# Seven block products for eight in a feed-forward projection: 8 of 22 tile pairs of the gate and up projections in Strassen's form

## The chip, the cores and the metric
The kernel runs on one core of one Trainium2 chip. The metric is the device time in microseconds of one execution. TensorE (PE) multiplies, with its weight loads shown as PEld; VectorE is DVE, ScalarE is ACT, GpSimd is POOL, and SyncE (SP) issues most of the DMA transfers.

## The reference
A token mixer block and a second block follow each other on 512 tokens of width 1024. The second block holds the two feed-forward layers that the change touches. For each:

```python
def swiglu(h, w_gu, w_down):
    gu = h @ w_gu                      # 1024 -> 2 x 2816
    g, u = jnp.split(gu, 2, axis=-1)
    return (jax.nn.silu(g) * u) @ w_down

f = swiglu(rmsnorm(h, ffn1_pre_g[l]), ffn1_w_gu[l], ffn1_w_down[l])
h = h + 0.5 * rmsnorm(f, ffn1_post_g[l])
```

Everything is float32. `rmsnorm(x, g)` multiplies x by the reciprocal root of its mean square plus 1e-6 and by the gain g.

## The kernel before
**Layout.** Features lie on the 128 partitions, the 512 tokens in the free dimension. A weight is cut into blocks of 128 by 128. All weights stream through *slots* of 8 blocks (`w_raw`, a ring of 6): a slot holds the blocks of one output tile of 128 features. SP loads slot c once slot c-6 has been used on PE (`s_used`).

**Three terms.** Each float32 product is made as three reduced ones: ACT copies a slot to its high part (`split_hi`, `w_hi`, a ring of 4, so it waits for the use of slot c-4), DVE subtracts for the low part, in place of the raw slot (`split_lo`, `w_lo`), and PE adds high by high, high by low and low by high (`gemm`). The tokens have such parts too (`act_hi`, `act_lo`: `HH`, `HL`). The rstd of a row is not in them: it is multiplied in when a tile leaves PSUM (`RP`, `pre_rstd`).

**The feed-forward layer.** `ffn1_up` has 44 slots: gate tile t is slot 2t, up tile t slot 2t+1, for t from 0 to 21. Slots 0 to 2 and half of 3 are multiplied while the boundary before still makes the tokens (`after_boundary`); from slot 4 on PE goes through the slots one by one, with four banks in turn (`ACC[0]`, `ACC[1]`, then `PS[0]`, `PS[1]`). After each tile DVE multiplies by the rstd (L1558), ACT applies silu to the gate tile (L911), DVE multiplies gate by up (L1564) into a ring of two, ACT makes the high part (L633) and DVE the low part (L1185) of the hidden tile. `ffn1_down`, 24 slots, reads them. The second layer (`ffn2`) is the same code.

**Order.** Each engine has its own queue, written out in program order, with semaphores between. DVE and ACT split each slot three slots ahead of PE (`AHEAD = HI_RING - 1`), in `stage`:

```python
for s in range(COUNT[name]):
    if s >= split and base + s + AHEAD < N_SLOTS:
        split_lo(base + s + AHEAD)
    m = tile_ended(name, s)
    if tile is not None and m is not None and (per is None or s % per == per - 1):
        if arrived is not None:
            dve.wait_ge(arrived, at + m + 1)
        tile(m if per is None else s // per)
```

`Chain.link` makes DVE wait until the instruction just issued has ended.

Of the kernel before, what the change touches and what calls it, by code (L numbers as in the profile page):

```python
# [8 lines left out]
F32 = mybir.dt.float32  # L9
F32R = mybir.dt.float32r  # L10
ACT = mybir.ActivationFunctionType
ALU = mybir.AluOpType
# [128 lines left out]
START = [(0, (0, 1, 2)), (1, (0, 1, 2)), (0, (3, 4)), (1, (3, 4)), (2, (0, 1, 2, 3, 4))]  # L141
START += [(s, (k,)) for k in range(5, DK) for s in range(TOGETHER)]


# [58 lines left out]
def block_program(nc, xT, mem_t, w_all, params, consts, rope, decay, w_gate, w_dt, w1k, w1v, w2k, w2v, out_t):  # L203
    ctx = ExitStack()
    with ctx:
# [104 lines left out]
        AH = place("ffn_hi", [P, FK, S], 32, F32R)  # L310
        AL = place("ffn_lo", [P, FK, S], 76, F32R)

        QKV = place("sb_qkv", [P, SB_RING * 3, S], 32)
# [285 lines left out]
        def _(act):  # L599
# [88 lines left out]

            def mixer_root(name, at):

                act.wait_ge(s_rsum, ROWS[name] + 1)
                for c in range(at.start, at.stop):
                    ins = A(RQ[:, c:c + 1], PS[5][:, c:c + 1], ACT.Sqrt, scale=1.0 / D, bias=EPA[:, c:c + 1])
                ins.then_inc(s_rroot, 1)

            def boundary(b, name, gain, next_gain, following):

                slots = tail_slots(name)
                post_root = mixer_root if name == "out2" else row_root
                post_root(f"post{b}", at=chunks(0))  # L700
# [50 lines left out]
            act.wait_ge(s_in, 48)  # L751
            A(WGH[:], WGR[:], ACT.Copy).then_inc(sem("gate_w_hi"), 1)
            row_root("pre")
# [150 lines left out]
            def ffn(n):  # L904
                up = f"ffn{n}_up"

                def tile(t):
                    if t % 2:
                        product_hi(PROD0[f"ffn{n}"] + t // 2, AH[:, t // 2, :])
                    else:  # L910
                        A(ev(up, t), ev(up, t), ACT.Silu).then_inc(sem("gate_made"), 1)  # L911
                stage(up, tile, 2, s_acc)
                branch(f"ffn{n}_down", f"g_ffn{n}_post")
# [3 lines left out]
            for s in range(COUNT["sb_qkv"]):  # L917
                if s >= 2:
                    split_hi(base + s + AHEAD)
                if s == 3:  # L920
                    act.wait_ge(s_late["dt_w"], 16)
                    A(WDH[:], WDR[:], ACT.Copy).then_inc(sem("dt_w_hi"), 1)
# [216 lines left out]
            ffn(2)  # L1139
            row_root("post4", at=chunks(0))  # L1140
            late_squares("ffn2_down")
            late_gains("ffn2_down", "g_ffn2_post")
            row_root("post4_late", at=chunks(1))


        @block.vector
        def _(dve):
# [187 lines left out]
            split_lo(3)  # L1335
            dve.wait_ge(sem("gate_w_hi"), 1)
            TT(WGL[:], WGR[:], WGH[:].bitcast(F32), ALU.subtract).then_inc(sem("gate_w_lo"), 1)
            row_rstd("pre")
# [72 lines left out]
            def first_maxima():  # L1411
# [13 lines left out]
                chain.link(V.memset(PTC[:], 0.0))  # L1425
                dve.wait_ge(sem("gate_rows"), 1)
                TT(NROWS[0:24, :], PS[5][0:24, :], RP[0:24, :], ALU.mult).then_inc(sem("gate_rows_copied"), 1)
                dve.wait_ge(sem("cmp_done"), 1)
# [125 lines left out]
            def ffn(n):  # L1554
                up = f"ffn{n}_up"

                def tile(t):
                    TT(ev(up, t), acc_bank(up, t)[:], RP[:], ALU.mult).then_inc(s_acc, 1)  # L1558
                    if t % 2:
                        j = PROD0[f"ffn{n}"] + t // 2  # L1560
                        free_product(j)
                        dve.wait_ge(sem("gate_made"), 2 * DK + (n - 1) * FK + t // 2 + 1)
                        dve.wait_ge(s_acc, TILE0[up] + t + 1)
                        TT(PR[:, j % 2, :], ev(up, t - 1), ev(up, t), ALU.mult).then_inc(s_pr, 1)  # L1564
                        low(j, AH[:, t // 2, :], AL[:, t // 2, :])
                stage(up, tile, split=2, arrived=s_used)
                branch(f"ffn{n}_down")
# [11 lines left out]
            for s in range(COUNT["sb_qkv"]):  # L1579
# [4 lines left out]
                if s == 4:  # L1584
                    V.memset(ACR[:].bitcast(F32), 0.0)
                    V.memset(SEL[:].bitcast(F32), 0.0)
                    dve.wait_ge(sem("dt_w_hi"), 1)
                    TT(WDL[:], WDR[:], WDH[:].bitcast(F32), ALU.subtract).then_inc(sem("dt_w_lo"), 1)
                if s == 6:
                    dve.wait_ge(sem("dt_rows"), 1)  # L1590
                    TT(NROWS[0:SSD_HEADS, :], PS[2][0:SSD_HEADS, :], RP[0:SSD_HEADS, :], ALU.mult).then_inc(
                        sem("dt_rows_copied"), 1)
                if s == 8:
# [259 lines left out]
        def _(pe):  # L1853
# [74 lines left out]

            def after_boundary(b, branch, name, between=None):

# [17 lines left out]
                row_spread(f"pre{b}", PS[3])  # L1948
                gemm(name, TOGETHER, HH, HL, half=1, h=1)
                for s in range(TOGETHER + 1, COUNT[name]):  # L1950
# [111 lines left out]
            def first_scores():  # L2062

                pe.wait_ge(sem("gate_w_lo"), 1)
                narrow_rows(5, WGH, WGL, 24, range(0, 2))
# [13 lines left out]
                ins.then_inc(sem("cmp_hidden"), 1)  # L2079
                narrow_rows(5, WGH, WGL, 24, range(7, DK)).then_inc(sem("gate_rows"), 1)  # L2080
                pe.wait_ge(sem("cmp_gelu"), 2)
# [8 lines left out]
                ins.then_inc(sem("cmp_done"), 1)  # L2090
                pe.wait_ge(sem("gate_rows_copied"), 1)
                token_major(5, 24).then_inc(sem("gate_psum"), 1)
# [92 lines left out]
            def ffn(n, entered, left, branch):  # L2185
                after_boundary(entered, branch, f"ffn{n}_up")
                down = f"ffn{n}_down"

# [6 lines left out]
            def dt_steps(s):  # L2195
                if s == 6:
                    pe.wait_ge(sem("dt_w_lo"), 1)
                    narrow_rows(2, WDH, WDL, SSD_HEADS).then_inc(sem("dt_rows"), 1)
                if s == 7:
                    pe.wait_ge(sem("dt_rows_copied"), 1)  # L2200
                    token_major(4, SSD_HEADS).then_inc(sem("dt_psum"), 1)
# [406 lines left out]
```

## Time and profile before

| what | value |
|---|---|
| median of 3 runs | 1956.94 us (1956.7 to 1958.17) |
| profiled execution, its own time | 1958.82 us |
| its span, first to last instruction | 1957.1 us |
| mean granted clock of TensorE | 0.997 |
| PE busy | 1916.5 us, 98% |
| DVE busy | 1110.1 us, 57% |
| ACT busy | 859.0 us, 44% |
| first feed-forward, up projection from slot 4 | starts at 589.69 us |

The span and the busy times are of one profiled execution. Matmuls are pipelined: their recorded durations overlap, so what one costs is read from the distance of the starts. The granted clock is a share of full speed.

### The profile page before, as it was taken

To read this page: it belongs to the slowest core of one execution; us is meant where nothing else is said; L and a number is where in the kernel's file an instruction comes from. 1 tells how busy PE (TensorE), PEld (TensorE's weight loads), DVE (VectorE), ACT (ScalarE), POOL (GpSimd) and SP (SyncE) were. 2 spreads that over 40 slices of the span, in tenths; PEclk is the share of its full clock that TensorE was granted. 3 is DMA by queue.
4 is the path that set the end of the run, shared out by engine and by line. 5 is a ranking of instruction groups with operands and counts; after the bars stand their busy time and mean duration, and the time that the engine had idled before them with its cause. 6 is when DMAs were issued, how large, how long until landed. Compare 5 with 4: busy or idle time off the path is not lost.

```text
span 1957.1 us, 25607 instructions
## 1 busy us (share of the span) xinstructions
PE 1916.5 (98%) x10256; PEld 1568.7 (80%) x10256; DVE 1110.1 (57%) x1825; ACT 859.0 (44%) x1532; POOL 91.1 (5%) x109
## 2 busy tenths in 40 slices
PE   8999999999999999999999999999999999999997
PEld 6688877888888888888878887878898888888886
DVE  5678845644465444422738989884745475444323
ACT  4355632533343222322527777974535453222321
POOL 0100000000020000000200000111200020000000
PEclk9999999999999999999999999999999999999999
DMA  7211122333323333333222221122252223333331
GB/s 277 67 55 45 54 70 61 88 99 89 101 63 111 96 97 94 91 90 91 89 80 71 65 66 54 55 87 87 56 157 89 78 86 97 97 91 90 92 96 62
DMA packets 49431, 170.53 MB, mean 87 GB/s; under 512 B 5520, under 2 KB 8080, under 8 KB 48928
## 3 DMA queue, kind: packets, MB, share of 16 engines
q1 hardware_dynamic: 48816, 166.73, 28.4%
q0 software_dynamic: 496, 2.16, 0.3%
q8 instruction: 81, 1.33, 0.3%
q14 instruction: 38, 0.31, 0.1%
HBM read 166.77 MB, written 2.10 MB: 86 GB/s over the span
## 4 chain that ended last, share of the span: by engine, by line
PE 87%; DVE 9%; ACT 2%; issue 1%; DMA 0%; SPq 0%; DVEq 0%
PE acc L1887 54%; PE bank L1887 19%; PE acc L2040 2%; PE bank L1976 2%; DVE w_lo L1160 1%; PE acc L2411 1%; PE bank L2253 1%; PE bank L2160 1%; PE bank L2224 1%; DVE bank L1240 1%; PE bank L2398 1%; PE bank L2432 1%; PE bank L2013 1%; DVE residual L1246 1%; PE bank L1901 1%
## 5 line engine op out<-in xcount | busy, mean ns | idle before, releaser
L1160 DVE TENSOR_TENSOR w_lo<-w_raw,w_hi 128x1024 fp32r<-128x1024 f32 (+2 forms) x306 | 366.5, 1199 | 327.9 <-ACT w_hi L609 327.4
L1887 PE MATMUL acc<-act_hi,w_hi 128*128 128x512 f32 (+1 forms) x1096 | 430.2, 393 | 17.4 <-DVE w_lo L1160 9.5
L1887 PE MATMUL acc<-act_lo,w_hi 128*128 128x512 f32 (+1 forms) x1096 | 419.4, 383 | 0.0
L1887 PE MATMUL acc<-act_hi,w_lo 128*128 128x512 f32 (+1 forms) x1096 | 416.5, 383 | 0.0
L609 ACT ACTIVATE w_hi<-w_raw 128x1024 fp32r<-128x1024 f32 (+2 forms) x306 | 314.5, 1029 | 192.7 <-PE acc L1887 162.7
L1887 PEld LDWEIGHTS acc<-act_hi,w_hi 128*128 128x128 f32 x1096 | 206.4, 188 | 64.5 <-issue 13.2
L1887 PEld LDWEIGHTS acc<-act_hi,w_lo 128*128 128x128 f32 x1096 | 205.9, 188 | 44.5 <-issue 1.2
L1887 PEld LDWEIGHTS acc<-act_lo,w_hi 128*128 128x128 f32 x1096 | 206.6, 189 | 43.1 <-issue 2.2
L1887 PE MATMUL bank<-act_hi,w_hi 128*128 128x512 f32 (+1 forms) x520 | 192.6, 370 | 1.2 <-DVE w_lo L1160 1.2
L1887 PE MATMUL bank<-act_hi,w_lo 128*128 128x512 f32 (+1 forms) x520 | 191.0, 367 | 0.0
L1887 PE MATMUL bank<-act_lo,w_hi 128*128 128x512 f32 (+1 forms) x520 | 190.9, 367 | 0.0
L1887 PE MATMUL acc<-ffn_hi,w_lo 128*128 128x512 f32 (+1 forms) x352 | 134.2, 381 | 0.0
L1887 PE MATMUL acc<-ffn_lo,w_hi 128*128 128x512 f32 (+1 forms) x352 | 134.2, 381 | 0.0
L1887 PE MATMUL acc<-ffn_hi,w_hi 128*128 128x512 f32 (+1 forms) x352 | 134.2, 381 | 0.0
L633 ACT ACTIVATE ffn_hi<-product 128x512 fp32r<-128x512 f32 x44 | 27.8, 632 | 195.4 <-DVE product L1564 195.4
L1887 PEld LDWEIGHTS bank<-act_hi,w_hi 128*128 128x128 f32 x520 | 97.8, 188 | 19.4 <-DVE w_lo L1160 1.4
L1887 PEld LDWEIGHTS bank<-act_lo,w_hi 128*128 128x128 f32 x520 | 97.8, 188 | 18.0 <-issue 0.2
L1887 PEld LDWEIGHTS bank<-act_hi,w_lo 128*128 128x128 f32 x520 | 97.8, 188 | 17.7
L1206 DVE TENSOR_TENSOR square_sum<-square_sum,evacuated 128x512 f32<-128x512 f32 (+1 forms) x47 | 31.1, 662 | 99.6 <-ACT evacuated L650 99.6
L911 ACT ACTIVATE evacuated<-evacuated 128x512 f32<-128x512 f32 x44 | 27.8, 632 | 121.7 <-DVE evacuated L1558 121.7
L1887 PEld LDWEIGHTS acc<-ffn_lo,w_hi 128*128 128x128 f32 x352 | 66.2, 188 | 14.1
L1887 PEld LDWEIGHTS acc<-ffn_hi,w_lo 128*128 128x128 f32 x352 | 66.2, 188 | 14.0
(471 smaller groups left out, 3128.9 us busy)
## 6 DMA issues: line engine op xcount, KB each, us to landing
w_raw<-w_all SPq DMA_DIRECT2D x282, 512.0 KB, 3.5
w_raw<-w_all SPq DMA_DIRECT2D x16, 384.0 KB, 3.2
residual<-xT SPq DMA_DIRECT2D x8, 256.0 KB, 8.4
cmp_w_k<-w1k SPq DMA_DIRECT2D x1, 2048.0 KB, 8.1
cmp_w_v<-w1v SPq DMA_DIRECT2D x1, 2048.0 KB, 12.3
w_raw<-w_all SPq DMA_DIRECT2D x8, 256.0 KB, 2.6
out_t<-residual SPq DMA_DIRECT2D x16, 128.0 KB, 1.7
ret_decay<-decay POOLq DMA_DIRECT2D x4, 256.0 KB, 3.3
```

The costliest lines, as they stand in the source:

```text
L609: A(WH[:, c % HI_RING, 0:nb * P], WR[:, c % RAW_RING, 0:nb * P], ACT.Copy).then_inc(s_hi, 1)
L633: A(dst, PR[:, j % 2, 0:n], ACT.Copy).then_inc(s_ph, 1)
L911: A(ev(up, t), ev(up, t), ACT.Silu).then_inc(sem("gate_made"), 1)
L1160: TT(WL[:, c % RAW_RING, 0:nb * P], WR[:, c % RAW_RING, 0:nb * P], WH[:, c % HI_RING, 0:nb * P].bitcast(F32), ALU.subtract).then_inc(s_lo, 1)
L1206: TT(SSQ[:, cols], SSQ[:, cols], ev(name, m)[:, cols], ALU.add).then_inc(s_fsq, 1)
L1240: STT(out=scaled_at(k), in0=FO[:, k, cols], scalar=factor, in1=PS[(4, 3)[h]][:, cols], op0=ALU.mult, op1=ALU.mult).then_inc(sem("branch_sc ...
L1246: TT(X[:, k, cols], X[:, k, cols], scaled_at(k), ALU.add).then_inc(s_x, 1)
L1887: ins = MM(bank[:, cols], w[:, at, k * P:(k + 1) * P], x, start=first and r == 0 and k == 0, stop=last and r == 2 and k == nb - 1)
L1901: ins = MM(PS[bank][:, c:c + 1], part[:, c * P:(c + 1) * P], ones[:, 0:1], start=j == 0, stop=j == len(parts) - 1)
L1976: ins = TR((V_BANK if bank is None else PS[bank])[:, to + c * P:to + (c + 1) * P], src[:, c * P:(c + 1) * P], ident)
L2013: ins = MM(PS[2 * branch + hh][:, 0:kw], QK[rows, p, i * P:(i + 1) * P], QK[rows, 5 + branch, 0:kw], start=True, stop=True)
L2040: ins = MM(out.rearrange("p (e f) -> p e f", e=2), a[:, k, at], w[:, ring:ring + 2, k * P:(k + 1) * P], start=r == 0 and k == 0, stop=r == ...
```

## The change
In each up projection, the pairs t = 4, 6, ..., 18 (gate tile t and up tile t) are computed as one 2 by 2 block product over pairs of neighbouring blocks of the inner dimension (even and odd), the gate and up tile, and the two halves of the tokens (256 each), with seven products where eight stand otherwise (Winograd's variant, with four sums of weights and four of tokens). The tokens' sums are made once per layer, the weights' sums for each of the 8 pairs; both get high and low parts. The seven accumulated products fill seven half banks of `PS[2]` to `PS[5]`, and DVE adds them up (`gathered`). The other 14 pairs stay as they were.

Besides: the hidden tiles aren't split at once; they are kept (`AP`), and their high and low parts are made after pair 19. The up tile is no longer multiplied by the rstd; to make up for it, the norm after the down projection takes its epsilon times the square of the root (`EPA`), a column at a time (`kept_root` for `row_root`). Some semaphores are shared under new names (`narrow_...`), which changes no work.

```diff
+FAST = range(4, 19, 2)
+FFN_SUMS = ["sub0", "low0", "sub1", "low1", "sub2", "low2", "sub3"] + [f"add{t}" for t in FAST]
+FFN_SUMS.insert(8, "low3")
...
+        AP = place("ffn_product", [P, FK, S], 76)
+        TH = place("token_sums_hi", [P, 4, 4, HALF], 32, F32R)
+        TR = place("token_sums", [P, 4, 4, HALF], 48)
+        SXH = place("weight_sums_hi", [P, 3, 4, P], 64, F32R)
+        XG = place("tokens_gained", [P, 2, S], 120)
...
# ACT, ffn(n)
+                def silu(t):
+                    act.wait_ge(s_acc, TILE0[up] + 2 * t + 1)
+                    A(ev(up, 2 * t), ev(up, 2 * t), ACT.Silu).then_inc(sem("gate_made"), 1)
+                def gained_tokens(k):
+                    for e in range(2):
+                        ins = A(XG[:, e, :], X[:, 2 * k + e, :], ACT.Copy, scale=par(f"g_ffn{n}_pre", 2 * k + e))
+                    ins.then_inc(scaled, 1)
+                def token_sums_hi(k):
+                    act.wait_ge(combined, ffn_sum(n, f"sub{k}"))
+                    A(TH[:, k], TR[:, k], ACT.Copy).then_inc(scaled, 1)
+                def weight_sums_hi(t):
+                    act.wait_ge(combined, ffn_sum(n, f"add{t}"))
+                    A(SXH[:], SX[t // 2 % 2][:], ACT.Copy)
+                def first_product(t):
+                    act.wait_ge(s_used, base + 2 * t + 2)
+                    A(FM[:], PS[2][:, 0:HALF], ACT.Copy).then_inc(scaled, 1)
...
+                silu(0)
+                gained_tokens(0)
+                split_hi(base + 5)
+                silu(1)
+                token_sums_hi(0)
+                gained_tokens(1)
+                split_hi(base + 6)
+                split_hi(base + 7)
+                silu(2)
+                for k in (1, 2):
+                    token_sums_hi(k)
+                    gained_tokens(k + 1)
+                token_sums_hi(3)
+                split_hi(base + 8)
+                weight_sums_hi(4)
+                split_hi(base + 9)
+                split_hi(base + 10)
+                silu(3)
+                for t in FAST:
+                    more = t + 2 in FAST
+                    split_hi(base + 2 * t + 3)
+                    first_product(t)
+                    split_hi(base + 2 * t + 4)
+                    if more:
+                        weight_sums_hi(t + 2)
+                    silu(t)
+                    split_hi(base + 2 * t + 5)
+                    split_hi(base + 2 * t + 6)
+                    silu(t + 1)
...
# DVE, ffn(n)
+                def gate(t):
+                    dve.wait_ge(s_used, base + 2 * t + 1)
+                    TT(ev(up, 2 * t), acc_bank(up, 2 * t)[:], RP[:], ALU.mult).then_inc(s_acc, 1)
+                def product(t):
+                    dve.wait_ge(s_used, base + 2 * t + 2)
+                    dve.wait_ge(sem("gate_made"), 2 * DK + (n - 1) * FK + t + 1)
+                    src = ev(up, 2 * t + 1) if t in FAST else acc_bank(up, 2 * t + 1)[:]
+                    TT(AP[:, t, :], ev(up, 2 * t), src, ALU.mult).then_inc(s_pr, 1)
...
+                def token_sums(k):
+                    dve.wait_ge(scaled, ffn_copy(n, f"scale{k}"))
+                    b11, b12, b21, b22 = [XG[:, e, tokens(h)] for e in range(2) for h in range(2)]
+                    chain.link(TT(TR[:, k, 0], b12, b11, ALU.subtract))
+                    chain.link(TT(TR[:, k, 1], b22, TR[:, k, 0], ALU.subtract))
+                    TT(TR[:, k, 2], b22, b12, ALU.subtract)
+                    TT(TR[:, k, 3], b21, TR[:, k, 1], ALU.subtract).then_inc(combined, 1)
...
+                def weight_sums(t):
...
+                    chain.link(TT(sums[:, 0], w21, w22, ALU.add))
+                    chain.link(TT(sums[:, 1], sums[:, 0], w11, ALU.subtract))
+                    TT(sums[:, 2], w12, sums[:, 1], ALU.subtract)
+                    TT(w21, w11, w21, ALU.subtract).then_inc(combined, 1)
...
+                def gathered(t):
+                    g, u, h0, h1 = ev(up, 2 * t), ev(up, 2 * t + 1), tokens(0), tokens(1)
+                    dve.wait_ge(scaled, ffn_copy(n, f"first{t}"))
+                    chain.link(TT(FU[:], FM[:], PS[3][:, h0], ALU.add))
+                    TT(g[:, h0], FM[:], PS[2][:, h1], ALU.add)
+                    TT(g[:, h1], FU[:], PS[3][:, h1], ALU.add)
+                    chain.link(TT(u[:, h0], FU[:], PS[4][:, h0], ALU.add))
+                    chain.link(TT(g[:, h1], g[:, h1], PS[4][:, h1], ALU.add))
+                    TT(g, g, RP[:], ALU.mult).then_inc(s_acc, 1)
+                    chain.link(TT(u[:, h1], u[:, h0], PS[3][:, h1], ALU.add))
+                    chain.link(TT(u[:, h0], u[:, h0], PS[5][:, h0], ALU.add))
...
+                STT(out=EPA[:], in0=RQ[:], scalar=EPS, in1=RQ[:], op0=ALU.mult, op1=ALU.mult)
+                gate(0)
+                product(0)
+                split_lo(base + 5)
+                gate(1)
+                token_sums(0)
+                split_lo(base + 6)
+                product(1)
+                token_sums_lo(0)
+                token_sums(1)
+                split_lo(base + 7)
+                gate(2)
+                token_sums_lo(1)
+                token_sums(2)
+                product(2)
+                token_sums_lo(2)
+                token_sums(3)
+                weight_sums(4)
+                token_sums_lo(3)
+                first_slot_lo(4)
+                weight_sums_lo(4)
+                gate(3)
+                for t in FAST:
+                    more = t + 2 in FAST
+                    product(t - 1)
+                    split_lo(base + 2 * t + 2)
+                    split_lo(base + 2 * t + 3)
+                    if more:
+                        weight_sums(t + 2)
+                    gathered(t)
+                    if more:
+                        first_slot_lo(t + 2)
...
+                    product(t)
+                    if more:
+                        weight_sums_lo(t + 2)
...
+                    gate(t + 1)
...
# PE
+                def fast_pair(t):
+                    c, s1, s2, s4 = SLOT0[up] + 2 * t, 0, 1, 2
+                    h0, h1 = tokens(0), tokens(1)
+                    pe.wait_ge(s_lo, c + 2)
+                    pe.wait_ge(sem("ffn_summed"), ffn_sum(n, "low3"))
...
+                    for k in range(4):
+                        e, o = 2 * k, 2 * k + 1
+                        for bank, at, opens, (w, wl), (x, xl) in (
+                                (2, h0, True, block(c, e), token(e, h0)), (2, h1, False, block(c, o), token(o, h0)),
+                                (3, h0, True, summed(s2, k), token_sum(k, 1)), (3, h1, False, summed(s1, k), token_sum(k, 0)),
+                                (4, h0, True, block(c + 1, e), token_sum(k, 2)), (4, h1, False, summed(s4, k), token(o, h1)),
+                                (5, h0, True, block(c + 1, o), token_sum(k, 3))):
+                            out = PS[bank][:, at]
+                            MM(out, w, x, start=opens and k == 0, stop=False, skip_group_check=True)
+                            MM(out, w, xl, start=False, stop=False, skip_group_check=True)
+                            ins = MM(out, wl, x, start=False, stop=k == 3, skip_group_check=True)
+                    ins.then_inc(s_used, 2)
```

After the loop both queues go through pairs 19 to 21 with the hidden parts of tiles 0 to 4, 5 to 9, 10 to 14 and 15 to 21 between their splits, gates and products. `token_sums_lo` and `weight_sums_lo` subtract the high parts of 1024 and 1536 elements; the latter then splits the pair's second slot, and `first_slot_lo` its first.

## Rows read from the trace of the kernel before

**Rows 1.** The page: busy time by engine, the chain's shares, one weight load.
```profile
PE 1916.5 (98%) x10256; PEld 1568.7 (80%) x10256; DVE 1110.1 (57%) x1825; ACT 859.0 (44%) x1532; POOL 91.1 (5%) x109
...
PE 87%; DVE 9%; ACT 2%; issue 1%; DMA 0%; SPq 0%; DVEq 0%
...
L1887 PEld LDWEIGHTS acc<-act_hi,w_hi 128*128 128x128 f32 x1096 | 206.4, 188 | 64.5 <-issue 13.2
```
**Rows 2.** Chain that ended last, entries of both layers: start us, us, what.
```profile
589.69 11.43 PE acc L1887 x48
601.12 11.20 PE bank L1887 x48
...
1596.66 11.44 PE acc L1887 x48
```
**Rows 3.** Busy time of a stretch with 256-column matmuls alone: us, engines, clock, DMA.
```profile
1445.30:1467.90 22.60, 22.60 (x193) 22.60 (x192) 10.45 (x9) 10.38 (x15) 0.00 (x0) 1.00 0.63 182
```
**Rows 4.** PE's timeline in the boundary before the first layer (24 such, two shown).
```profile
582.43 0.28 PE L1887 MATMUL acc<-act_hi,w_hi 128*128 128x256 f32 x1
...
585.15 0.28 PE L1887 MATMUL bank<-act_hi,w_lo 128*128 128x256 f32 x1
```
**Rows 5.** DVE's timeline: entry of the first layer, and two 256-element instructions.
```profile
588.85 1.29 DVE L1558 TENSOR_TENSOR evacuated<-acc,pre_rstd 128x512 f32<-128x512 f32 x2 [0.21 <-ACT pre_rstd L725]
...
593.25 1.23 DVE L1160 TENSOR_TENSOR w_lo<-w_raw,w_hi 128x1024 fp32r<-128x1024 f32 x1 [0.26 <-ACT w_hi L609]
594.39 0.68 DVE L1558 TENSOR_TENSOR evacuated<-bank,pre_rstd 128x512 f32<-128x512 f32 x1
...
597.87 0.68 DVE L1558 TENSOR_TENSOR evacuated<-bank,pre_rstd 128x512 f32<-128x512 f32 x1
598.68 0.69 DVE L1564 TENSOR_TENSOR product<-evacuated 128x512 f32<-128x512 f32 x1
...
1941.58 0.41 DVE L1246 TENSOR_TENSOR residual<-residual,bank 128x256 f32<-128x256 f32 x1
1942.10 0.43 DVE L1240 SCALAR_TENSOR_TENSOR bank<-branch_out,bank 128x256 f32<-128x256 f32 x1
```
**Rows 6.** ACT's timeline: entry of the first layer, and a root of two columns.
```profile
588.84 1.28 ACT L911 ACT_TABLE_LOAD   x1
...
599.47 0.63 ACT L633 ACTIVATE ffn_hi<-product 128x512 fp32r<-128x512 f32 x1 [2.77 <-DVE product L1564]
600.00 1.04 ACT L609 ACTIVATE w_hi<-w_raw 128x1024 fp32r<-128x1024 f32 x1
...
1938.31 0.17 ACT L642 ACTIVATE row_root<-bank 128x2 f32<-128x2 f32 x1 [1.01 <-PE bank L1901]
```
**Rows 7.** ACT's groups by form: count, busy us, mean ns, idle before.
```profile
L705 ACT ACTIVATE act_hi<-residual,param_cols 128x256 fp32r<-128x256 f32 x64 | 32.5, 508 | 39.0 <-DVE residual L1246 38.9
...
L708 ACT ACTIVATE residual_squares<-residual 128x256 f32<-128x256 f32 x64 | 25.7, 402 | 0.0
```
**Rows 8.** The page: issues of the slots' loads, KB, median us to landing.
```profile
w_raw<-w_all SPq DMA_DIRECT2D x282, 512.0 KB, 3.5
```
**Rows 9.** Stretches of 1 us: PE, PEld, DVE, ACT, POOL busy, granted clock, DMA.
```profile
1216.00:1217.00 1.00, 0.11 (x2) 0.00 (x0) 1.00 (x2) 0.98 (x2) 0.00 (x0) 1.00 0.00 0
...
1220.00:1221.00 1.00, 1.00 (x13) 1.00 (x12) 0.96 (x2) 0.00 (x0) 0.00 (x0) 0.50 0.00 0
...
1222.00:1223.00 1.00, 1.00 (x8) 0.87 (x8) 1.00 (x2) 0.86 (x2) 0.00 (x0) 1.00 0.00 0
```
**Rows 10.** PE's timeline at the start of the kernel.
```profile
9.04 0.77 PE L1887 MATMUL acc<-act_hi,w_hi 128*128 128x512 f32 x1 [9.04 <-DVE w_lo L1160]
...
12.36 0.63 PE L1887 MATMUL acc<-act_hi,w_hi 128*128 128x512 f32 x1
12.79 0.60 PE L1887 MATMUL acc<-act_lo,w_hi 128*128 128x512 f32 x1
...
14.42 0.39 PE L1887 MATMUL acc<-act_lo,w_hi 128*128 128x512 f32 x1
```

More of the change, by code:

```diff
@@ L142, with ffn_sum, ffn_copy @@
 START += [(s, (k,)) for k in range(5, DK) for s in range(TOGETHER)]
+FAST = range(4, 19, 2)
+FFN_SUMS = ["sub0", "low0", "sub1", "low1", "sub2", "low2", "sub3"] + [f"add{t}" for t in FAST]
+FFN_SUMS.insert(8, "low3")
+FFN_COPIES = [f"{what}{k}" for k in range(4) for what in ("scale", "hi")] + [f"first{t}" for t in FAST]
+def ffn_sum(n, what):
+    return (n - 1) * len(FFN_SUMS) + FFN_SUMS.index(what) + 1
+def ffn_copy(n, what):
+    return (n - 1) * len(FFN_COPIES) + FFN_COPIES.index(what) + 1
 BEFORE_STATES = 6
@@ L751, in _ @@
             act.wait_ge(s_in, 48)
-            A(WGH[:], WGR[:], ACT.Copy).then_inc(sem("gate_w_hi"), 1)
+            A(WGH[:], WGR[:], ACT.Copy).then_inc(sem("narrow_w_hi"), 1)
             row_root("pre")
@@ L905, in ffn @@
                 up = f"ffn{n}_up"
[L907 to L912, printed above, removed]
+                base, j0 = SLOT0[up], PROD0[f"ffn{n}"]
+                scaled, combined = sem("ffn_copied"), sem("ffn_summed")
+                def silu(t):
+                    act.wait_ge(s_acc, TILE0[up] + 2 * t + 1)
+                    A(ev(up, 2 * t), ev(up, 2 * t), ACT.Silu).then_inc(sem("gate_made"), 1)
@@ L913, in ffn @@
+                last = FAST[-1]
+                split_hi(base + 2 * last + 7)
+                silu(last + 2)
+                hidden_hi(*range(0, 5))
+                split_hi(base + 2 * last + 8)
+                hidden_hi(*range(5, 10))
+                split_hi(base + 2 * last + 9)
+                silu(last + 3)
+                hidden_hi(*range(10, 15))
+                split_hi(base + 2 * last + 10)
+                hidden_hi(*range(15, FK))
                 branch(f"ffn{n}_down", f"g_ffn{n}_post")
@@ L1566, in ffn @@
-                stage(up, tile, split=2, arrived=s_used)
+                base, j0 = SLOT0[up], PROD0[f"ffn{n}"]
+                scaled, combined = sem("ffn_copied"), sem("ffn_summed")
+                def gate(t):
[6 more added lines that the diff above has]
+                    TT(AP[:, t, :], ev(up, 2 * t), src, ALU.mult).then_inc(s_pr, 1)
+                    dve.wait_ge(s_pr, j0 + t + 1)
+                    V.sem_inc(s_acc, 1)
@@ new lines, in token_sums_lo @@
+                def token_sums_lo(k):
+                    dve.wait_ge(scaled, ffn_copy(n, f"hi{k}"))
+                    TT(TL[:, k], TR[:, k], TH[:, k].bitcast(F32), ALU.subtract).then_inc(combined, 1)
+                def weight_sums(t):
+                    c, sums = base + 2 * t, SX[t // 2 % 2]
+                    if t == FAST[0]:
+                        dve.wait_ge(combined, ffn_sum(n, "sub3"))
+                    for slot in (c, c + 1):
+                        dve.wait_ge(s_raw[slot % RAW_RING], 16 * (slot // RAW_RING + 1))
+                    w11, w12, w21, w22 = [WR[:, slot % RAW_RING, :].rearrange("p (k e m) -> p e k m", k=4, e=2)[:, e]
+                                          for slot in (c, c + 1) for e in range(2)]
+                    chain.link(TT(sums[:, 0], w21, w22, ALU.add))
+                    chain.link(TT(sums[:, 1], sums[:, 0], w11, ALU.subtract))
+                    TT(sums[:, 2], w12, sums[:, 1], ALU.subtract)
+                    TT(w21, w11, w21, ALU.subtract).then_inc(combined, 1)
@@ new lines, in ffn @@
+                last = FAST[-1]
+                split_lo(base + 2 * last + 6)
+                product(last + 1)
+                split_lo(base + 2 * last + 7)
+                gate(last + 2)
+                hidden_lo(*range(0, 5))
+                split_lo(base + 2 * last + 8)
+                product(last + 2)
+                hidden_lo(*range(5, 10))
+                split_lo(base + 2 * last + 9)
+                gate(last + 3)
+                hidden_lo(*range(10, 15))
+                split_lo(base + 2 * last + 10)
@@ L1567, in ffn @@
+                product(last + 3)
+                hidden_lo(*range(15, FK))
                 branch(f"ffn{n}_down")
@@ L1927, in tail, with after_boundary @@
                     slot(s, h=1)
-            def after_boundary(b, branch, name, between=None):
+            def after_boundary(b, branch, name, between=None, rest=None):
                 for h in range(2):
@@ L1949, in after_boundary @@
                 gemm(name, TOGETHER, HH, HL, half=1, h=1)
+                if rest is not None:
+                    rest()
+                    return
                 for s in range(TOGETHER + 1, COUNT[name]):
@@ L2079, in first_scores @@
                 ins.then_inc(sem("cmp_hidden"), 1)
[L2080 removed]
+                narrow_rows(5, WGH, WGL, 24, range(7, DK)).then_inc(sem("narrow_rows"), 1)
                 pe.wait_ge(sem("cmp_gelu"), 2)
@@ L2189, in slot, with pairs @@
+                def pairs():
+                    for t in range(2, FK):
+                        if t in FAST:
+                            fast_pair(t)
+                        else:
+                            gemm(up, 2 * t, HH, HL)
+                            gemm(up, 2 * t + 1, HH, HL)
+                after_boundary(entered, branch, up, rest=pairs)
                 def slot(s, **how):
```

84 lines of the change are left out of this document (55 added, 29 removed).

## The prediction
> **What bounds the kernel now.** I read the page first: TensorE (PE) is busy for 98% of the span, VectorE (DVE) for 57%, ScalarE (ACT) for 44%, and the chain that ended last is 87% PE [rows 1]. Then the chain of waits at the entry of the first feed-forward block: from 589.69 us on it is PE alone, in blocks of 48 matmuls and 11.20 us [rows 2]. In this stage, then, 1 us of PE work saved is 1 us of the kernel, as long as nothing holds PE. Last I read the timelines of DVE and ACT there, for what a saved multiplication would cost them.
>
> **What a fast pair saves on PE.** An ordinary pair is 2 slots of 8 blocks with 3 terms: 48 matmuls of 512 columns. 11.20/48 = 0.2333 us from start to start [rows 2]. A fast pair is 4 block rows of 7 products with 3 terms: 84 matmuls of 256 columns. Such matmuls follow each other at 22.60/193 = 0.117 us with the weight load always busy [rows 3], and in the boundary before this stage, where the bank changes every three or six matmuls as it will here, at (585.15 - 582.43)/23 = 0.118 us [rows 4]. I take 0.1186, so 9.96 us, and a gain of 1.24 us a pair; 8 pairs give 9.9 us in each of the two blocks, 19.8 us in all. Bounds of the pitch: 0.117 from the window, and 0.188 if the load of each weight block were not overlapped [rows 1], which is 15.8 us a pair. Both rows nearest in form are at the low end.
>
> **Durations for the rest.** DVE needs 0.69 us for 512 elements and 1.23 for 1024 [rows 5]; I take 0.41 for 256 and 1.77 for 1536 (one more step of 0.54). The next instruction that waits for nothing starts before the end: two of 512 take 1.29, so 0.60 from start to start, and 1.14 for 1024 (593.25 to 594.39); in proportion 0.33 for 256 and 1.68 for 1536. One that waits for the one before it starts later than its end: 0.81 for 512 (597.87 to 598.68) and 0.52 for 256 (1941.58 to 1942.10). I use 0.54 for the latter. ACT: 0.63 for 512 (0.54 to the next start), 1.04 for 1024 (by the same overlap 0.95), so 1.46 for 1536 (1.37); a scale held in a column adds 0.1 at 256 elements (0.508 against 0.402), so 0.73 for 512, and a pair of them 1.28 to the next start or 1.37 to the end [rows 6, 7].
>
> **Removed and added work.** Per ordinary pair DVE loses one multiplication by the rstd row and one low part, and ACT one high part, but the 22 hidden high and low parts only move to the end. Added on DVE per block: four token sums of 1.74 us (0.54 + 0.54 + 0.33 + 0.33), their low parts of 1.14; for each fast pair weight sums of 2.82 (0.81 + 0.81 + 0.60 + 0.60), their low part of 1.68 and the gathering of about 4.0 (five waits on itself at 0.54, two free ones at 0.33, one of 512 at 0.60). ACT gets eight scaled copies, the high parts of the sums and a copy of a half bank.
>
> **Where it lies on the path: the entry.** PE reaches the first fast pair after pairs 2 and 3, at 612.16 if nothing holds it (589.69 with two blocks of 11.2, and 0.07 of first start). Before that, DVE and ACT must make all token sums and the first weight sums, each in program order, and they hand work to each other all the time, because the scaled tokens have one buffer and gate(t), silu(t) and the splits stand between. I walk it in the first block from 588.85, where the rstd row is ready [rows 5]:
> ACT loads its table until 590.12 [rows 6]; silu(0) 0.54, scaled tokens 0 1.28, high part of slot 5 1.04: 592.99. DVE: low part 1.14, gate(1) 0.60: 594.77. Token sums 0 end at 596.6; ACT: high part 0.95, scaled tokens 1 1.28, high part of slot 6 1.04: 599.92. DVE: low part of slot 6 ends at 601.19. PE wanted that slot at 600.96, and starts at 601.3 (0.15 after, as its 589.69 stands to the end of the first gate, 588.85 + 0.69 [rows 2, 5]): 0.4 us late.
> DVE from 601.10: product(1) 0.81, low sums 0 1.14, token sums 1 1.74, low part of slot 7 1.14, gate(2) 0.69: 606.62. ACT: silu(2) 0.54, high sums 1 0.95, scaled tokens 2 1.37: 609.5. DVE: token sums 2 1.82 (to the end): 611.4. ACT: high sums 2 0.95, scaled tokens 3 1.37: 613.75. DVE: token sums 3 1.82, a wait on itself 0.12: 615.7; weight sums 2.91: 618.64. ACT: their high part 1.37, high part of slot 9 1.04: 621.10. DVE: low sums 1.68, low part of slot 9 1.23: 624.04. PE starts at 624.2, where 612.5 was possible. That is a stall of 11.7 us, 12.1 with the 0.4 before. The second block begins in the same way (its chain starts with the same piece, 48 matmuls in 11.44 us [rows 2]). The slots of weights need no part of this: they land 3.5 us after issue [rows 8] and are released pairs ahead.
>
> **The clock behind the stall.** The trace has a gap in mid-run: PE is nearly idle in 1216 to 1217 (and in the next microsecond), the granted clock is 0.50 in 1220 and 1.00 again in 1222 [rows 9]. At the start of the kernel, after idleness, 512-column matmuls follow each other at 0.43 us (12.36 to 12.79) and last 0.63, and from 14.42 on they last 0.39 [rows 10]; the first one starts at 9.04. So work goes on at half clock (1.2 of 2.4 GHz) for some 3.3 us after the gap and for some 4.4 us at the start, and where 256 columns take 0.43/2 = 0.213 for 0.1186 us it costs 0.44 of that time: 1.5 to 1.9 us. A stall of 11.7 us is far longer than that gap; I take 1.8 us a block. The Trainium skill (TensorE: Matmul & The Clock Gate, "HAM oscillation — how this bites in real kernels") says the same: a wait between bursts of matmuls sends the array back to half rate, and the cost is paid at every such wait. By that rule, the trace agrees; without it the kernel would come out 3.6 us earlier.
>
> **Steady state.** After fast pair t ends at F: copy on ACT to F+0.65, gathering to F+4.6, low part of slot 2t+4 1.14, product(t) 0.81, low weight sums 1.68, low part of the next slot 1.23: F+9.5. PE asks at F+11.2, after the ordinary pair. Margin 1.7 us: no stall. The ACT parts (high part, 1.37, silu, high part) end by F+5.2. The weight sums of t+2 wait for a slot that lands 3.5 us after the previous pair's end, and are done at about 6.4 us of the fast pair's 9.96. If gathering and sums were 1.7 us slower the cover is gone. The Trainium skill (VectorE: DVE Perf Modes, "The DRAIN you can't avoid") says that a DVE instruction keeps the next one back until its pipeline is empty, waits or none. Rows 5 show 0.60 from start to start for 0.69 of duration, so it does not hold for these. By that rule each free successor costs 0.09 more, some 1.5 us a block, and the sum would be 1968.
>
> **The end of the block.** After pair 18 DVE and ACT have three ordinary pairs (33.6 us) for 15.2 and 13.9 us of hidden low and high parts beside 11 us of splits, gates and products. Walked the same way, the last low part is made at about F+41.4, and PE asks for it at F+48. Nothing waits. The root per column in place of one instruction for two columns (0.17 [rows 6]) is one more small instruction in four places, two of them at the very end: 0.2 us.
>
> **Sum.** Per block: -9.9 + 0.4 + 11.7 + 1.8 = +4.0 us. Two blocks +8.0, roots +0.2. The profiled execution has a span of 1957.1 and took 1958.8; the median of the runs, 1956.9, lies at the span. So 1956.9 + 8.2 = 1965.
>
> **Unknown sizes.** Weight sums read blocks of 128 out of a slot with gaps: between 0.60 (no cost) and 1.14 (twice the elements' time) each, 0 to 1.9 us a block at the entry; I take 0, since no read of DVE in the rows pays for its place. Scaled copies: 0.54 to 0.73, six on the walk, -0.6 to 0. Half clock 0 to 1.9. The forecast's own range is then 1960 to 1970.
>
> **Rivals.** (A) The handing over costs little, and DVE's own work decides: it has 26.1 us from 588.9 on, 27.4 with the table load, so 616.4 against 612.2. With the half clock: -9.9 + 4.3 + 1.8 = -3.8 a block, 1949. It would need ACT's results ahead of DVE everywhere; for it speaks that ACT has only about 18 us of work there, against it the single buffer. The sign turns where the whole delay before the first fast pair is under 8.1 us. (B) The steady state overruns its 1.7 us of margin: each further us is paid at 7 pairs of 2 blocks, +14, 1979. (C) A fast pair's matmuls are bound by the weight load: even at 0.133 us nothing is saved (11.2/84), and at 0.188 the kernel takes 1965 + 16 x 5.8 = 2058; rows 3 and 4 speak against it. (D) The clock doesn't fall, or the walk is a few us too long: 1961 down to 1955.
>
> **How the numbers follow.** Forecast 0.60, A 0.14, B 0.10, C 0.02, D 0.14. Less than 0.2% (3.9 us) is what a measurement can't tell from no change: 1953 to 1961. Faster: A and a little of D, 0.17. Same: most of D and the forecast's low end, 0.14. Slower: 0.69. For 8 in 10 the range reaches from A's 1948 to 1972.
>
> **What would show it.** Right: PE idle for 11 to 12 us ahead of the first fast pair in each block, released by the low part (w_lo) on DVE; granted clock 0.5 behind it; no other wait of PE in the stage; 84 matmuls in 9.96 us; a second block like the first. Wrong: a wait ahead of every fast pair, matmuls of 0.13 us or more from start to start, or a stall below 8 us.

## The result and the profile after

The changed kernel takes 1965.16 us (median of 6, 1963.83 to 1966.05) against 1958.06 for the kernel before (6 runs): ratio 1.0037, 95% interval 1.0024 to 1.005. It is slower, by 7 us where 8 were forecast, and for the reason forecast. (Only one execution in what follows was in a slow state, 2281.46 us at a mean granted clock of 0.768, in the run with seven pairs from 6 on, walked; its ratio leaves that one out.)

Less work and a longer span, from the page (answers to [rows 1]):

```profile
span 1964.3 us, 27025 instructions
...
PE 1902.9 (97%) x10832; PEld 1589.1 (81%) x10832; DVE 1204.8 (61%) x2015; ACT 904.9 (46%) x1592; POOL 90.5 (5%) x109
...
PE 84%; DVE 11%; ACT 3%; issue 2%; DMA 0%; SPq 0%; DVEq 0%; ACTq 0%
```

PE is busy 13.6 us less, the span is 7.2 us longer. Who keeps PE waiting, over the whole span (us in total, times, longest):

```profile
PE bank L2419 <- DVE w_lo L1249: 21.2, 2, 10.6
PE acc L2087 <- DVE w_lo L1249: 9.2, 2, 9.0
...
PE acc L2087 <- DVE evacuated L1650: 0.3, 2, 0.2
```

L2419 is the first matmul line of `fast_pair`. It waits twice, once in each layer, for 10.6 us, on DVE's low part; the other fourteen fast pairs wait for nothing. (The 9.0 is the kernel's start.) What came before the wait in the first layer, on DVE:

```profile
599.57 1.23 DVE L1249 TENSOR_TENSOR w_lo<-w_raw,w_hi 128x1024 fp32r<-128x1024 f32 x1 [3.30 <-ACT w_hi L636]
...
607.74 1.23 DVE L1670 TENSOR_TENSOR token_sums_lo<-token_sums,token_sums_hi 128x1024 fp32r<-128x1024 f32 x1 [1.65 <-ACT token_sums_hi L947]
...
611.77 1.23 DVE L1670 TENSOR_TENSOR token_sums_lo<-token_sums,token_sums_hi 128x1024 fp32r<-128x1024 f32 x1 [0.53 <-ACT token_sums_hi L947]
...
619.95 1.76 DVE L1692 TENSOR_TENSOR weight_sums_lo_a<-weight_sums_a,weight_sums_hi 128x1536 fp32r<-128x1536 f32 x1 [0.23 <-ACT w_hi L636]
621.62 1.22 DVE L1249 TENSOR_TENSOR w_lo<-w_raw,w_hi 128x1024 fp32r<-128x1024 f32 x1
...
642.23 1.22 DVE L1249 TENSOR_TENSOR w_lo<-w_raw,w_hi 128x1024 fp32r<-128x1024 f32 x1
```

The brackets are DVE's idle time ahead of the instruction, each ended by a result of ACT. The last low part before the first fast pair ends at 622.8; in the loop, the one for pair 6 ends at 643.4, and PE asks for it at 645.8. The chain of waits after the first fast pair (answers to [rows 2]; the ordinary pairs, x48, with a fast pair in each gap):

```profile
634.58 11.20 PE bank L2087 x48
655.72 11.20 PE bank L2087 x48
676.85 11.20 PE bank L2087 x48
```

21.13 to 21.14 us for one ordinary and one fast pair, so 9.94 us for the fast one. The granted clock (us of the stretch, PE busy, PEld, DVE, ACT, POOL, clock, DMA; answers to [rows 9]):

```profile
612.00:614.00 2.00, 0.32 (x2) 0.00 (x0) 1.93 (x4) 0.96 (x2) 0.00 (x0) 1.00 0.34 84
...
618.00:620.00 2.00, 0.00 (x0) 0.00 (x0) 1.77 (x3) 2.00 (x3) 0.00 (x0) 0.50 0.00 0
...
624.00:625.00 1.00, 1.00 (x7) 1.00 (x7) 0.69 (x1) 1.00 (x2) 0.00 (x0) 0.50 0.00 0
...
627.00:628.00 1.00, 1.00 (x10) 1.00 (x10) 1.00 (x2) 0.00 (x0) 0.00 (x0) 1.00 0.00 0
```

PE works at half clock (1.2 of 2.4 GHz) from 622.9 to about 626. The first fast pair takes 11.68 us (622.90 to 634.58) in place of 9.94. In the second layer it takes 12.96, with half clock for longer (stretches of PE alone):

```profile
1624.00:1634.00 10.00, 0.24 (x1) 0.61 0.15 52
1634.00:1638.00 4.00, 4.00 (x20) 0.50 0.00 0
```

Where the 7 us came in, from the starts of the row sums (a few single-column matmuls that stand in both programs):

| row sums | before | after | difference |
|---|---|---|---|
| ahead of the first feed-forward layer | 585.27 | 585.17 | -0.1 |
| behind it | 930.78 | 932.98 | +2.2 |
| in the mixer, first | 1286.11 | 1288.35 | +2.2 |
| in the mixer, next | 1317.36 | 1321.15 | +3.8 |
| ahead of the second layer | 1592.25 | 1596.03 | +3.8 |
| behind it | 1937.77 | 1945.11 | +7.3 |

The first layer adds up: 8 x (11.20 - 9.94) = 10.1 saved, against 10.6 of wait, 1.7 by which the first fast pair is slower than the others, and 0.1 by which slot 4 starts later behind the row sums (4.48 us behind them, in place of 4.42; this is the wait of 0.2 for DVE's first evacuation, which the table of waits shows twice): +2.3, as in the table. The second: -10.1 + 10.6 + 3.0 + 0.1 = +3.6, as in the table (7.34 - 3.78). The 1.5 us in the mixer belong to no changed instruction. There PE has gaps of 0.73 and 1.26 us in both kernels; after the second, this execution of the changed kernel shows matmuls at half clock, 0.43 us from start to start:

```profile
1311.82 1.29 PE L2602 MATMUL bank<-ssd_xbc,ssd_states 128*128 128x128 f32 x6 [1.26 <-DVE ssd_states L1977]
1312.77 0.77 PE L2087 MATMUL acc<-sb_hi_c,w_hi 128*128 128x512 f32 x1
1313.34 0.63 PE L2087 MATMUL acc<-sb_lo,w_hi 128*128 128x512 f32 x1
1313.76 0.63 PE L2087 MATMUL acc<-sb_hi_c,w_lo 128*128 128x512 f32 x1
```

In that of before they run at full clock behind the same gap, 0.23 us from start to start:

```profile
1309.59 0.94 PE L2358 MATMUL bank<-ssd_xbc,ssd_states 128*128 128x128 f32 x6 [1.26 <-DVE ssd_states L1777]
...
1310.60 0.39 PE L1887 MATMUL acc<-sb_lo,w_hi 128*128 128x512 f32 x1
1310.83 0.40 PE L1887 MATMUL acc<-sb_hi_c,w_lo 128*128 128x512 f32 x1
```

### The profile page after: what moved, and what is told of

It reads as the page before. It is cut to its first block, busy times and chain, and to the rows that moved or that the text cites. A ratio compares the mean times of both kernels' runs of the same rounds, so it can differ in the third digit from the quotient of the medians.

```text
span 1964.3 us, 27025 instructions
## 1 busy us (share of the span) xinstructions
PE 1902.9 (97%) x10832; PEld 1589.1 (81%) x10832; DVE 1204.8 (61%) x2015; ACT 904.9 (46%) x1592; POOL 90.5 (5%) x109
## 4 chain that ended last, share of the span: by engine, by line
PE 84%; DVE 11%; ACT 3%; issue 2%; DMA 0%; SPq 0%; DVEq 0%; ACTq 0%
PE acc L2087 44%; PE bank L2087 17%; PE bank L2419 3%; PE bank L2420 3%; PE bank L2421 3%; PE acc L2243 2%; PE bank L2179 2%; DVE w_lo L1249 2%; PE acc L2655 1%; PE bank L2497 1%; PE bank L2363 1%; ACT w_hi L636 1%; PE bank L2468 1%; DVE bank L1329 1%; PE bank L2642 1%
## 5 line engine op out<-in xcount | busy, mean ns | idle before, releaser
L2087 PE MATMUL acc<-act_hi,w_hi 128*128 128x512 f32 (+1 forms) x840 | 329.2, 392 | 17.2 <-DVE w_lo L1249 9.2
L2087 PE MATMUL acc<-act_lo,w_hi 128*128 128x512 f32 (+1 forms) x840 | 318.3, 379 | 0.0
L2087 PE MATMUL acc<-act_hi,w_lo 128*128 128x512 f32 (+1 forms) x840 | 315.8, 380 | 0.0
L2087 PEld LDWEIGHTS acc<-act_hi,w_hi 128*128 128x128 f32 x840 | 158.6, 189 | 52.1 <-issue 13.2
L2087 PEld LDWEIGHTS acc<-act_hi,w_lo 128*128 128x128 f32 x840 | 157.9, 189 | 33.0 <-issue 1.2
L2087 PEld LDWEIGHTS acc<-act_lo,w_hi 128*128 128x128 f32 x840 | 158.8, 189 | 31.8 <-issue 2.2
L2087 PEld LDWEIGHTS acc<-ffn_hi,w_hi 128*128 128x128 f32 x352 | 66.1, 188 | 14.1
L955 ACT ACTIVATE first_product<-bank 128x256 f32<-128x256 f32 x16 | 6.1, 383 | 143.8 <-PE bank L2421 143.8
```

The source lines that it names most:

```text
L2087: ins = MM(bank[:, cols], w[:, at, k * P:(k + 1) * P], x, start=first and r == 0 and k == 0, stop=last and r == 2 and k == nb - 1)
```

## The experiments

The theory: both entries cost 10.6 us of stall and 1.7 to 3.0 us of a slow first pair, put down to half clock, against 10.1 us that eight fast pairs save in each layer; nothing else of the change matters. The rivals: the late hidden parts and the roots cost something; the slow first pair isn't the clock; DVE's own work, not the handing over, makes the stall; the loop is at its limit.

The edits below are shortened. hi(s) and lo(s) stand for `split_hi(base + s)` and `split_lo(base + s)`, gained(k) for `gained_tokens(k)`, sums, sums_hi and sums_lo for the token sums and their parts, wsums, wsums_hi and wsums_lo for the weight sums; the renumbering of semaphores is left out.

**All pairs ordinary, the rest of the change kept.**

```diff
-FAST = range(4, 19, 2)
+FAST = ()
+LAST = 18
 # ACT, DVE: in place of everything ahead of the hidden parts
+for s in range(40):            # DVE: 39
+    if s >= 2: split_hi(base + s + 3)
+    if s % 2 == 0: silu(s // 2)   # DVE: gate(s // 2), else product(s // 2)
```

> Only the other parts of the change are left: all 22 pairs are ordinary, the hidden parts are made late and the up tile is read from PSUM without the rstd, with one root per column. Theory (the stall at the entry and the half clock behind it are the whole loss): no stall, PE goes through 40 slots of 5.6 us, so the time of before plus the small roots, 1958 (1957 to 1959). Rival (the late hidden parts or the roots cost something that the fast pairs hide): 1960 or more, PE waiting at the first slots of the down projection.

Measured 1959.26 us, ratio to before 1.0003 (0.9994 to 1.0012): just above the range, and by no more than the interval can't tell from no change. PE waits for nothing in either feed-forward stage but the 0.2 us at slot 4, and from the row sums ahead of a layer to those behind it take 345.59 us in place of 345.51. So the late hidden parts and the product out of PSUM cost 0.1 us a layer. What is slower must come with the fast pairs.

**PE kept busy during its wait.** The matmuls write a half bank that nothing uses.

```diff
 def fast_pair(t):
+    if t == FAST[0]:
+        for _ in range(86):
+            MM(PS[5][:, h1], HH[:, 0, 0:P], HH[:, 0, h1], start=True, stop=True, skip_group_check=True)
     pe.wait_ge(s_lo, c + 2)
```

> The changed kernel with 86 matmuls of 256 columns (86 x 0.1186 = 10.2 us) into an unused half bank ahead of the first fast pair, where PE waits 10.6 us in the changed kernel. They compute nothing that is used. Theory: the wait stays (it then shows as work), the granted clock stays at 1.00, and the two first fast pairs take 9.94 us where they took 11.68 and 12.96: 4.8 us less, 1960 (1959.5 to 1961.5). Rival (the slower first pair is not the clock but a wait on weights or the first use of banks): 1965 as the changed kernel.

Measured 1960.3 us, ratio 1.0008 (0.9999 to 1.0018). The half clock is gone (stretches of PE alone, then the chain):

```profile
612.00:622.00 10.00, 10.00 (x86) 1.00 0.19 54
...
624.00:628.00 4.00, 4.00 (x37) 1.00 0.00 0
```
```profile
622.67 0.39 PE bank L2422
...
632.89 11.19 PE bank L2087 x48
```

The first fast pair takes 10.22 us (622.67 to 632.89) in place of 11.68, and in the second layer 10.22 (1630.40 to 1640.62) in place of 12.96. So the clock is worth 1.5 + 2.7 = 4.2 of the 7 us, won by keeping PE at senseless work alone. The other 0.28 us over 9.94 are not the clock: a fast pair that PE had to wait for pays them at full clock too (10.21 us in the second layer of the start at 6, below). By the medians this kernel is 1.9 us above before and the changed one 7.1; what lies between 4.2 and these 5.2 us isn't in the two pairs. (The trace of this run has no half clock behind the gaps in the mixer.)

**The scaled tokens all buffered, ACT making them early; DVE's order kept.**

```diff
-        XG = place("tokens_gained", [P, 2, S], 120)
+        XG = place("tokens_gained", [P, DK, S], 104)
 # ACT
-silu(0) gained(0) hi(5) silu(1) sums_hi(0) gained(1) hi(6) hi(7) silu(2) sums_hi(1) gained(2) sums_hi(2) gained(3) sums_hi(3)
+silu(0) gained(0) hi(5) silu(1) gained(1) sums_hi(0) hi(6) hi(7) gained(2) gained(3) sums_hi(1) silu(2) sums_hi(2) sums_hi(3)
```

> The changed kernel (first fast pair 4) with a buffer for all scaled tokens and ACT's order changed to make them early; DVE's order and work stay. Theory of the hand to hand: the waits of DVE on scaled tokens go, walked with the measured durations the first fast pair is ready at 620.3 in place of 622.9, so the stall is 8 us in place of 10.6, the half clock stays: 1965 - 5.2 = 1960 (1958 to 1962). Rival (the single buffer is the whole stall, and DVE's own work fits): stall under 4 us, 1951 or less. Rival (it costs nothing, DVE's work alone decides): 1965.

Measured 1959.13 us, ratio 1.0005 (0.9995 to 1.0015).

```profile
PE bank L2420 <- DVE w_lo L1250: 15.3, 2, 7.6
```

7.6 us of wait in each layer in place of 10.6: the walk had given 8. The buffer and ACT's order were changed together, so it is the two of them that take 3 us off the stall; the other 7.6 are DVE's work and the waits that remain (5.7 us of DVE's idle time in place of 8.4).

**Seven pairs, starting at 6.** My first order for it alternates the sums with two more ordinary pairs, with the single buffer.

```diff
-FAST = range(4, 19, 2)
+FAST = range(6, 19, 2)
 # ACT
+... silu(3) sums_hi(2) gained(3) hi(10) sums_hi(3) hi(11) silu(4) hi(12) wsums_hi(6) hi(13) hi(14) silu(5)
 # DVE
+... gate(3) sums(2) lo(10) product(3) sums_lo(2) sums(3) lo(11) gate(4) sums_lo(3) wsums(6) product(4) lo(12) wsums_lo(6) gate(5)
```

> Seven fast pairs, 6 to 18, in place of eight: the same token sums and first weight sums with the same single buffer, but two more ordinary pairs (22.4 us of PE) to hide them. Theory: DVE gets 3.7 us more of ordinary work per pair, so the first fast pair is ready about 7.4 us later than 622.9, at 630.3, and due at 634.6: no stall, no half clock, 7 x 1.26 x 2 = 17.6 us below before: 1940 (1938 to 1943). Rival (a fast pair saves less than 1.26 us in the steady state, or each pair after the first has a small wait): above 1945.

Measured 1947.65 us, ratio 0.9947 (0.993 to 0.9963): faster than before, but 7 us above the forecast. I had added DVE's work to the old ready time and not walked the new order. DVE waits for ACT again and again in it:

```profile
PE bank L2434 <- DVE w_lo L1256: 4.9, 2, 2.4
```

2.4 us of wait in each layer. In the first, half clock follows it (PE alone):

```profile
634.00:636.00 2.00, 0.01 (x1) 1.00 0.47 90
636.00:638.00 2.00, 1.57 (x12) 0.94 0.42 172
638.00:640.00 2.00, 2.00 (x11) 0.50 0.00 0
640.00:642.00 2.00, 2.00 (x15) 0.71 0.00 0
```

In the second it doesn't, behind the same wait:

```profile
1638.00:1640.00 2.00, 0.88 (x7) 1.00 0.66 227
1640.00:1642.00 2.00, 2.00 (x19) 1.00 0.00 0
```

The first fast pair takes 11.74 us in the one and 10.21 in the other. With the wait, the entries cost 4.2 and 2.7 us.

**Seven pairs from 6 on, walked.** All tokens buffered; on each engine the next split comes ahead of work that needs the other engine's newest result (`hi(5)` before `gained(0)`, `hi(7) gained(2) gained(3) hi(8)` in a row; on DVE `lo(7) sums(1) gate(2) sums_lo(1)`).

> Seven fast pairs from 6 on, as in the run that started at 6 and lost 2.4 us and the clock at each entry, but with all scaled tokens buffered and an order in which no engine waits for the other's newest result; walked, the first fast pair is ready at 628 and due at 634. Theory (the entry's order is all that was wrong there, and a fast pair saves 1.26 us each): 7 x 1.26 x 2 = 17.6 us below before, 1940.5 (1939 to 1942), 7 us below the other start at 6 and 2.5 us above eight pairs without a stall. Rival (the seven pairs save less for another reason): 1945 or more.

Ratio 0.9917 (0.9897 to 0.9936), which is 1942.1 us beside the 1958.39 of before, at the upper end of the range; no fast pair waits in the profile (span 1940.5). So order and buffer together were worth some 5.5 us. Seven pairs save 16.3 of the 17.6 us forecast, which the interval (12.5 to 20.2) takes in; in the trace each layer takes 336.72 us in place of 345.51, 8.8 less, as forecast.

**Eight pairs, 5, 7, ..., 19.** One more ordinary pair (11.2 us of PE) ahead of the first fast one, one less behind the last. All scaled tokens are buffered, and the order is walked: three changes at once.

```diff
-FAST = range(4, 19, 2)
+FAST = range(5, 20, 2)
 # ACT
+silu(0) hi(5) gained(0) hi(6) silu(1) gained(1) sums_hi(0) hi(7) gained(2) gained(3) hi(8) sums_hi(1) silu(2) hi(9) sums_hi(2) hi(10) silu(3) sums_hi(3) wsums_hi(5) hi(11) hi(12) silu(4)
 # DVE
+gate(0) product(0) lo(5) gate(1) sums(0) lo(6) product(1) sums_lo(0) lo(7) sums(1) gate(2) sums_lo(1) lo(8) sums(2) product(2) gate(3) sums_lo(2) lo(9) sums(3) wsums(5) product(3) sums_lo(3) lo(10) wsums_lo(5) gate(4)
 # behind the loop, DVE
+lo(44) product(20) hidden(0-2) lo(45) hidden(3,4) gate(21) hidden(5-12) lo(46) product(21) hidden(13-21)
```

> Eight fast pairs again, 5, 7, ..., 19, and a buffer for all scaled tokens, with ACT making them as early as it can; only pairs 20 and 21 are left for the late hidden parts, whose order is spread anew. Walked with the measured durations the first fast pair is ready at 620.5 and due at 623.3. Theory: no stall, 8 x 1.26 x 2 = 20.2 us below before: 1938 (1936 to 1941). Rival (DVE's own work is what stalls PE, with the hidden parts now short of time): a stall of some us at the first fast pair or at the down projection, 1943 or more.

Measured 1937.91 us, ratio 0.9896 (0.9881 to 0.9911). It beats both kernels, by 20 and by 27 us. No fast pair waits. DVE's last low part for the first fast pair, and PE's blocks around it:

```profile
618.30 1.22 DVE L1249 TENSOR_TENSOR w_lo<-w_raw,w_hi 128x1024 fp32r<-128x1024 f32 x1
```
```profile
611.85 11.20 PE acc L2086 x48
...
632.98 11.20 PE acc L2086 x48
```

Ready at 619.5, due at 623.05, and the first fast pair takes 9.93 us at once (623.05 to 632.98).

**The same with the single buffer.**

```diff
-        XG = place("tokens_gained", [P, DK, S], 104)
+        XG = place("tokens_gained", [P, 2, S], 120)
 # ACT
+silu(0) hi(5) gained(0) hi(6) silu(1) sums_hi(0) gained(1) hi(7) hi(8) sums_hi(1) gained(2) silu(2) hi(9) sums_hi(2) gained(3) ...
```

> The version with fast pairs 5, 7, ..., 19, with the single buffer of the changed kernel for the scaled tokens and the rest of the order kept. Theory (it is the order of the two queues and the one more ordinary pair that hide the sums; the buffer matters only in the changed kernel's order): walked, ready at 621 and due at 623, 1938 as with all tokens buffered (1937 to 1940). Rival (the single buffer is what makes the two engines wait for each other in any order): a stall of 2 to 5 us and half clock in each layer, 1945 to 1953.

Measured 1938.48 us, ratio 0.9898 (0.9884 to 0.9913). The buffer doesn't matter once the order is right and there is one more pair to hide behind. The later start and the order aren't told apart: no run has one without the other. An estimate for this order with the first fast pair at 4: in the eight-pair run the last low part is ready 30.3 us behind the start of slot 4 (589.21); without the 3.7 us of DVE's work for one ordinary pair that is 26.6, and PE would ask for it at 22.6. Some 4 us of stall would be left.

**The loop's margin.** After each gathering, n chained additions of 256 elements.

```diff
                     gathered(t)
+                    for _ in range(3):        # 8 in the second kernel
+                        chain.link(TT(FX[:], RP[:, 0:HALF], RP[:, 0:HALF], ALU.add))
```

> The changed kernel with three chained DVE additions of 256 elements (3 x 0.46 = 1.4 us, written to an unused place) behind the gathering of each fast pair. In the changed kernel the last low part is made 2.3 us before PE asks for it. Theory (the steady state has that margin): the time of the changed kernel, 1965 (1963.5 to 1966.5). Rival (DVE sets the pace already in the loop): 1.4 us for each of 7 pairs in 2 layers, 1985.

Measured 1964.68 us, ratio 1.0033 (1.0021 to 1.0045), as the changed kernel. 1.4 us more of DVE in each pair cost nothing; PE's waits are the same two, 21.1 us.

> The same with eight additions (8 x 0.46 = 3.7 us) in each fast pair. Theory: 1.4 us over the margin of 2.3 at seven pairs of each of two layers, 14 x 1.4 = 19.6: 1984 (1978 to 1990), with a wait of PE for the low part ahead of each fast pair. Rival (margin much larger than 2.3, because the granted schedule shifts): 1965. Rival (none): 14 x 3.7 = 52 us, 2017.

Measured 1989.77 us in one run.

```profile
PE bank L2422 <- DVE w_lo L1250: 40.7, 16, 10.6
```

All 16 fast pairs wait now. The 14 later ones wait 40.7 - 21.2 = 19.5 us in all, 1.4 each, as forecast from a margin of 2.3 (3.7 - 2.3). From one fast pair's start to the next (647.47 to 670.27) it is 22.80 us in place of 21.14, so each costs 1.66: the waits and 0.26 around them. 14 x 1.66 = 23 of the 25 us; the slow first pair of its first layer takes 0.9 more than in the changed kernel's trace (12.62 for 11.68).

## Why the prediction was right

**The gain.** 1.24 us a pair was forecast from the pitch of 256-column matmuls; it is 11.20 - 9.94 = 1.26. Rival C is out: with a weight load ahead of each matmul, PE still issues one every 0.118 us.

**The stall.** The walk gave 11.7 us after a tile 0.4 us late; it was 10.6. The 0.4 didn't come: the low part of slot 6 was ready at 600.80, 0.3 us before PE wanted it at 601.08, where 601.19 had been walked. Its steps came in the order forecast: the low part of slot 6 waited 3.30 us for ACT, the low token sums 1.65 and 0.53, the weights' 0.23. The terms mis-sized: scaled copies 1.23 us a pair to the next start (forecast 1.28); a token sum's chain 0.45 a link (0.54); the weight sums 0.72 a link (0.81). The last two were taken from instructions that wait for another semaphore besides that of the one ahead; in the sums the next one starts 0.02 to 0.04 us after the end, and no run shows why it is shorter. Ten such links and four scaled copies make 1.1 of the 1.3 us by which PE started earlier (622.9 for 624.2). The weight sums' reads with gaps cost nothing (0.69 us), the 1536-element parts 1.76 and 1.48, as extrapolated (1.77 and 1.46).

**The clock.** 1.8 us a layer was forecast; 1.5 and 2.7 are the clock's by the busy-PE run, and 0.3 in each layer is a slow first start at any clock, which the sum left out. That the stall and the clock together outweigh the gain was right; the busy-PE run shows the share: stall alone, the kernel is level with before (1960.3, 1.0008). The rule of the Trainium skill (TensorE: Matmul & The Clock Gate) that a wait between bursts puts the array back to half rate agrees with both entries here. Not at every wait, though: of the two waits of 2.4 us in the start at 6, half clock follows one and not the other.

**The loop and the end.** Forecast: ready at F+9.5, margin 1.7. Measured: 643.4 - 634.58 = 8.9, margin 2.3, and the two runs with extra additions put it between 1.4 and 3.7. Rival B is out. For the roots 0.2 us were forecast; the run without fast pairs lies 0.8 us above before by its medians (interval from 1.2 below to 2.4 above), and can't tell 0.2 from nothing.

**Rival A** (DVE's own work decides) fails for this order: DVE is idle for 8.4 of the 34 us up to the last low part, behind ACT, and the stall is 10.6 us, not 4.3. But its place was right: what is left of the stall yields to an order without waits and one ordinary pair more. The rule that a DVE instruction holds back the next until it is drained (Trainium skill, VectorE: DVE Perf Modes, "The DRAIN you can't avoid") doesn't hold for these instructions: 593 to 622 on DVE is full of starts 0.33 us apart for durations of 0.42, and the kernel came out at 1965, not above. The prediction gave half of that section: it also says that a next instruction that isn't held starts earlier, and with that the trace agrees.

**Rival D** (no half clock, or a walk that is a few us too long) is out as a whole and true in a small part: the clock fell in both entries, and the walk was 1.1 us too long besides the 0.4.

**The sum** was +8.2 us; the medians give +7.1, the profiled executions +7.2. In these 7.2 there are 1.5 us in the mixer, behind gaps that both kernels have, and +5.9 from the two layers, +2.3 and +3.6, where +4.0 each were forecast. So the mechanism and its sign are as forecast, and part of the closeness is luck: a stall that was walked 1.5 us too long in each layer, a slow first pair that was taken 1.2 us too short in the second, and the 1.5 us of the mixer. How many of the other executions have these isn't known.

## What to carry to other kernels

A saved multiplication is worth its matmuls only if what feeds it is ready: walk the two queues that make its operands, instruction by instruction, to the first use, since the sum of the work (26 us here) and the last result (34 us) differ by the waits of one on the other. Where a stage starts with new preparatory work, start the cheap form later: one pair later and with the splits ahead of dependent work, eight pairs went from 7 us slower to 20 us faster than before. Count a stall of TensorE with the half clock behind it: here 10.6 us cost 12.3 and 13.6, and 2.4 us cost 4.2 with half clock behind it and 2.7 without.

## What was not expected of the hardware

The half clock doesn't last the same each time: 10.6 us of wait cost 1.5 us of it in the first layer and 2.7 in the second, in one execution. The run with all tokens buffered has 2.7 and 2.3 behind 7.6 us of wait, the one with three additions 2.0 and 2.3 behind 10.6. So the clock's share doesn't follow the length of the stall in these traces.

Short gaps bring it on in some executions and not in others. Behind the gaps of 0.73 and 1.26 us in the mixer, with 16 matmuls between, 5 of the 11 traces show half clock. Behind gaps of 0.4 and 1.8 us that all of them have earlier between the two layers (in the kernel before, at 1218 us) 7 of the 11 do. The trace of the run without fast pairs has neither, that of the changed kernel both. Each is worth 1.3 to 1.7 us, about the spread of a kernel's runs here (1956.7 to 1958.3, 1963.8 to 1966.1). What decides between them isn't settled. A difference of 1.5 us between two profiles should be looked for in the granted clock first.
